# Odd weight units of the later experts issued by ScalarE instead of SP

## The reference

```
def swiglu(h, w1, w3, w2):
    return (jax.nn.silu(h @ w1) * (h @ w3)) @ w2

def moe_swiglu(h, w_router, w1, w3, w2):
    ...
    for e in range(N_EXPERTS):
        y = y + combine[:, e:e + 1] * swiglu(xt, w1[e], w3[e], w2[e]).astype(jnp.float32)
```

## Time and profile before

| | |
|---|---|
| median of 3 runs | 1173.23 us (1171.65 to 1173.63) |
| the profiled execution's own time | 1173.44 us |
| its span, first to last instruction | 1171.5 us |
| PE busy | 1093.9 us (93%) |
| DVE, ACT, POOL busy | 328.6 us, 236.7 us, 39.4 us |
| read from HBM | 414.09 MB |
| issues of expert weights | 195, all by SP |

### The profile page before, as it was taken

The page is one execution under the profiler, slowest core; times in us unless marked ns, Lnnn a source line. Parts: engine busy times, 40 slices in busy tenths (PEclk is TensorE's granted clock), DMA queues, the critical chain, the costliest instruction groups (busy, mean ns, idle before and its releaser), DMA issues.

```text
span 1171.5 us, 25180 instructions
## 1 busy us (share of the span) xinstructions
PE 1093.9 (93%) x11721; PEld 626.0 (53%) x11721; DVE 328.6 (28%) x435; ACT 236.7 (20%) x370; POOL 39.4 (3%) x35
## 2 busy tenths in 40 slices
PE   7999999999999999999989969899997889999776
PEld 6888888889763354354446315344632434364234
DVE  4655555458660030040021004002200310040023
ACT  5676555656620000000000000000000000000002
POOL 3000000011000000000000000000000000000000
PEclk9999999999999999999999999999999899999988
DMA  9985656533379999999999999999999999999994
GB/s 347 387 294 191 203 182 202 191 126 142 134 305 402 422 382 424 428 420 426 424 428 422 426 428 420 427 425 427 421 426 426 424 423 426 427 422 425 426 424 166
DMA packets 58562, 417.88 MB, mean 357 GB/s; under 512 B 5730, under 2 KB 11924, under 8 KB 34004
## 3 DMA queue, kind: packets, MB, share of 16 engines
q1 hardware_dynamic: 56656, 411.21, 86.3%
q0 software_dynamic: 1440, 4.46, 1.0%
q10 hardware_dynamic: 356, 0.54, 0.1%
HBM read 414.09 MB, written 2.10 MB: 355 GB/s over the span
## 4 chain that ended last, share of the span: by engine, by line
PE 70%; DMA 26%; DVE 3%; ACT 1%; SPq 0%; issue 0%; DVEq 0%
PE psum L865 26%; DMA weights<-in_moe_w 26%; PE psum L903 15%; PE psum L771 8%; PE psum L772 8%; PE psum L773 8%; DVE hid_t L1715 1%; DVE sil L1713 1%; PE psum L986 1%; PE psum L844 0%; PE psum L779 0%; DMA x_res<-in_x 0%; PE psum L1107 0%; PE psum L880 0%; PE psum L1084 0%
## 5 line engine op out<-in xcount | busy, mean ns | idle before, releaser
L865 PE MATMUL psum<-weights,xg 128*32 128x512 f32 (+1 forms) x5072 | 494.4, 549 | 47.0 <-DMA weights<-in_moe_w 47.0
L865 PEld LDWEIGHTS psum<-weights,xg 128*32 128x32 f32 x5072 | 181.2, 111 | 357.9 <-issue 321.6
L903 PE MATMUL psum<-weights,hid_t 128*32 128x256 f32 x4480 | 247.1, 380 | 12.4 <-DVE hid_t L1715 8.3
L903 PEld LDWEIGHTS psum<-weights,hid_t 128*32 128x32 f32 x4480 | 151.4, 110 | 104.7 <-issue 13.7
L1713 DVE TENSOR_TENSOR sil<-sil,psum 128x1536 f32<-128x1536 f32 (+3 forms) x16 | 21.1, 1321 | 494.2 <-PE psum L865 493.5
L1567 DVE TENSOR_TENSOR low<-raw,high 128x2048 fp32r<-128x2048 f32 x50 | 114.3, 2286 | 95.5 <-ACT high L1271 95.3
L1271 ACT ACTIVATE high<-raw 128x2048 fp32r<-128x2048 f32 x51 | 97.8, 1917 | 51.8 <-PE psum L773 51.0
L1337 ACT ACTIVATE y_hi<-psum 128x768 fp32r<-128x768 f32 (+1 forms) x7 | 5.0, 719 | 489.4 <-PE psum L903 489.4
L771 PE MATMUL psum<-high,a_hi 128*128 128x512 f32 x224 | 87.2, 389 | 0.9 <-DVE a_lo L1604 0.9
L773 PE MATMUL psum<-low,a_hi 128*128 128x512 f32 x224 | 87.2, 389 | 0.0
L772 PE MATMUL psum<-high,a_lo 128*128 128x512 f32 x224 | 87.1, 389 | 0.0
(11 more groups left out here) (244 smaller groups left out, 662.0 us busy)
## 6 DMA issues: line engine op xcount, KB each, us to landing
weights<-in_moe_w SPq DMA_DIRECT2D x128, 1792.0 KB, 35.1
weights<-in_moe_w SPq DMA_DIRECT2D x47, 2048.0 KB, 37.1
raw<-in_ffn_w SPq DMA_DIRECT2D x42, 1024.0 KB, 7.2
weights<-in_moe_w SPq DMA_DIRECT2D x16, 1024.0 KB, 37.1
raw<-in_w_q SPq DMA_DIRECT2D x4, 1024.0 KB, 5.2
raw<-in_w_o SPq DMA_DIRECT2D x4, 1024.0 KB, 5.0
weights<-in_moe_w SPq DMA_DIRECT2D x4, 512.0 KB, 35.0
x_res<-in_x SPq DMA_DIRECT2D x2, 512.0 KB, 5.3
```

Source lines behind the costliest of these rows:

```text
L865: mm = pe.matmul(UP[c][g * BLK:(g + 1) * BLK, r, :], xg[:, k_, r * BLK:(r + 1) * BLK], w[:, g], start=k_ == 0, stop=k_ == DT - 1)
L903: mm = pe.matmul(Y[g * BLK:(g + 1) * BLK, to, :], hid_t[c][:, r, at_:at_ + BLK], w[:, b, g * GW:(g + 1) * GW], start=i == 0 and b == 0 and ...
```

## The change

From e1 on ScalarE issues the odd units (1, 3, ..., 21), except 21 of e7, on its own queue, and SP skips them. SP keeps e0 whole, the even units, and the last two units of e7. ScalarE issues in two lists for each place e: before the Silu of e those units that become free while TensorE uses the units up to 6 of e, and after the two Silus those that become free by the end of e. Each load waits for the same count of `unit_used` as before, and each list first reads the expert's number from `slot_expert`.

```
+def on_scalar_queue(e, j):
+
+    return e >= 1 and j % 2 == 1 and not (e == E - 1 and j >= MU - 2)
+
+
+def freed_between(first, last):
+
+    return [(n // MU, n % MU) for n in range(E * MU)
+            if on_scalar_queue(n // MU, n % MU) and first < MOE_FREED[n] - U_MOE <= last]
...
                 for j, key in enumerate(MOE_UNITS):
+                    if not ps.block and on_scalar_queue(e, j):
+                        continue
...
+            def load_odd_units(ps, first, last):
+
+                who_of = {}
+                for e, j in freed_between(first, last):
+                    if e not in who_of:
+                        act.wait_ge(slots_known, 1)
+                        who_of[e] = act.value_load(slot_expert[0:1, e:e + 1], min_val=0, max_val=E - 1)
+                    act.wait_ge(unit_used, ps.freed(j, e))
+                    cols = slice(0, moe_size(j))
+                    act.dma_start(expert_tile(ps, j, e, cols),
+                                  expert_source(who_of[e], *MOE_UNITS[j], cols)).then_inc(moe_landed[j], 16)
+
             def expert_feed_forward(ps, e):
                 ps.later(act, e, take_previous)
                 nb = ps.blocks(e)
+                if not ps.block:
+                    load_odd_units(ps, e * MU, e * MU + 7)
                 act.wait_ge(hidden_lo, ps.chunks(0, e))
...
+                if not ps.block:
+                    load_odd_units(ps, e * MU + 7, (e + 1) * MU)
```

## The result

The changed kernel took 1177.26 us in the median of 6 runs (1175.88 to 1177.91), the kernel before 1172.98. The ratio is 1.0042, with a 95% interval of 1.0031 to 1.0052: slower by 4.3 us between these medians, a small change but clear of noise. Forecast was 1179.0 us, that is 5.8 more than before. One of the six runs of before, at 1885.08 us, was disturbed and is left out of the ratio; without it the median of before is 1172.73. The profiled execution took 1177.91 us with a span of 1176.1, 4.6 more than before's.

A forecast was written before the change was run, and what follows sets the result against it. The prediction took the full DMA (share 1.01) to bound the expert part. Issue cost and rate counted nothing; late units added 5.8 us to the profiled 1173.44, giving 1179.2, or 1179.0 us against the median; range 1171.0 to 1187.0 us.

The forecast's parts named there:

- What bounds the kernel: Expert part, 425 to 1125 us: DMA share 1.01, TensorE 57 us to spare; end is landing of units 14, 15 plus 35.8 us.
- ScalarE's work at no cost: ScalarE's queue: 76 issues, 25 us in all over 740 us, and 21 reads of the expert's number, costed at nothing.
- The rate unchanged: Weight loads from 425 to 1125 us: DMA share stays 1.01 and rate 425 GB/s, within some 0.5%; no change in time.
- faster rival: Weight loads: two queues reach 428 GB/s and order holds, 5.1 us less, 1168.1 us; chance of faster 0.14.
- rival three: Weight loads: alternating queues costs what mixing with gathers cost, up to 8.7 us on top of 5.8, up to 1187.7; chance 0.13.
- rival one: Whole kernel: nothing measurable, 1173.2 us within 2.3; needs unit 14 at most 2.3 us late, 16 at most 6.5; chance 0.20.
- Unit 16 late, and so the end: End of the last expert: ScalarE's later units overtake SP's even ones, end 5.8 us later, bounds nothing to 9.8; chance 0.53.
- if both land before 16, it is late by 9.8 us: Last expert's w2: units 17 and 19 land before 16, at 1138.85 instead of 1129.05 us; TensorE ends 5.6 us later.
- unit 14 is overtaken by 17, and by part of 19: End of the last expert's w3: 17 and a quarter of 19 (1.2 us) overtake 14; pair and end 6.1 us later.
- The signs named: Changed profile: SP's units land after 40 us or more, ScalarE's 10 to 25; unit 14 about 1130, last w2 about 1139.
- How the lead arises: Weight queues: SP has 2.1 MB more per place, ScalarE gains one unit, 4.9 us, each; up to 20 us after four places.

The follow-up runs named there:

- e1: Not a run: the second expert place in the kernel, after the one SP keeps whole; the change's ScalarE loads begin here.
- run with 74 loads on ScalarE: The changed kernel with units 17 and 19 of the last expert back on SP's queue; 1171.89 us, ratio to before 0.9998; its rate was 423 GB/s.
- run with e7 alone: Against the kernel before, ScalarE takes the odd units of the last expert only, 10 loads instead of the change's 76; 1179.74 us, ratio 1.0068.
- changed kernel's second profile: The changed kernel run once more, unaltered, beside two others on the same chip; 1176.93 us, ratio to before 1.0034.
- e2: Not a run: the third expert place in the kernel, the one straight after e1; its units 0 and 1 were issued at 500.20 us.
- strict alternation: The changed kernel with odd and even units swapping queues from one expert to the next, so two units in a row are never SP's; 1175.05 us, ratio 1.0027.

## Why the prediction was right, and where it wasn't

**What bounds the kernel** held: DMA share 1.01 after as before, and the end set by what follows the last loads that TensorE must wait for.

**ScalarE's work at no cost** held. Silu waits for TensorE as before, and no wait of TensorE for Silu stands in the changed kernel's profile from 425 us to the end of the experts. The run with 74 loads on ScalarE costs nothing beyond its interval, which shows it. In the run with e7 alone TensorE does wait 0.88 us for a Silu, but that Silu waited for TensorE, not behind a load.

**The rate unchanged** held within its 0.5%: 424 against 425 GB/s, and the run with 423 had before's time. Neither the faster rival nor rival three came true. That spreading doesn't help the rate, as the Trainium skill has it (DMA: Bandwidth & Descriptors, rules for kernel authors), agrees with these rows; that it leaves the time alone, which I made rival one from it, doesn't: the order of landing, with what the clock did behind it, costs 4.3 us.

**Unit 16 late, and so the end** held in direction and place. Three sizes were off.

First, "if both land before 16, it is late by 9.8 us": unit 19 didn't, it landed 3.7 us after 16, so 16 was late by 6.0. Less 4.2 of slack this is a w2 start 1.85 us later, not 5.6. (The prediction also has 19 released after unit 10 is used; it is after unit 9, which ended at 1101.8 us before, just ahead of the issue of 19 at 1101.97.)

Second, "unit 14 is overtaken by 17, and by part of 19": the pair came 1.1 us late, not 6.1, since 17 was only partly there at 1125.3. In both the sum has all of 17 land ahead of 14, as if ScalarE's queue held nothing else by then. Unit 15, on the same queue, landed only at 1119.6, and 17 took 24.7 us from issue to landing.

Third, a term was missing: the wait for 16 was followed by the lower clock, 2.72 us in the profiled execution. The pair, on the other hand, which before ran at the lower clock for part of its 8.08 us, took 6.22 now; that gained nothing, since TensorE had to wait for 16.

So the forecast's size was in part luck. The sum of the profiled parts, 4.57 us, is near the 5.8 because a term too large and a missing one partly cancel. What is more, the prediction's own condition for rival one was met in this execution: unit 14 no more than 2.3 us late (1.1) and 16 no more than 6.5 (6.0). By lateness alone it would have lost 1.85 us, which the prediction counts as nothing measurable. In the changed kernel's second profile the shares are others, 3.10 us of later start and 1.69 of slower matmuls; lateness varies from one execution to the next.

**The signs named** came in part. Unit 14 was the later of the pair, and TensorE waited for each second unit. But SP's units took 30.0 us, not 40 or more, for the prediction didn't reckon with TensorE's later releases; the pair landed at 1125.3 and not near 1130, and w2 started at 1135.12 and not near 1139.

**How the lead arises** was half wrong. "After some four places the odd units are there up to 20 us early" takes the 2.1 MB per place for the source and asks for time. In e1, from 445 to 480 us, the two queues were still level, at 14.0 and 15.5 us. The change has the lead at the second place already: of the two loads issued at 500.20 us, units 0 and 1 of e2, SP's, behind the two halves of unit 22, took 38.5 us and ScalarE's 26.8.

```profile
weights<-in_moe_w SPq DMA_DIRECT2D x4, 1792.0 KB, 14.0
weights<-in_moe_w ACTq DMA_DIRECT2D x4, 1792.0 KB, 15.5
...
weights<-in_moe_w SPq DMA_DIRECT2D x1, 1792.0 KB, 38.5
weights<-in_moe_w ACTq DMA_DIRECT2D x1, 1792.0 KB, 26.8
```

What a queue holds when a load is issued decides, as the run with e7 alone shows. The unequal division is one way to make the queues unequal, and strict alternation ends it (30.2 against 29.6 us).

None of the kernels tried is faster than before beyond the interval.

## What to carry to other kernels

Where one queue already keeps the DMA engines full and a consumer takes the transfers in order, a single queue delivers them in that order; in these runs a second queue brought no more bytes in the same time and moved later units ahead of the one that was waited for. Look at the end of the stream: count which later transfers can overtake the last ones that are followed by compute alone, and compare with the slack of that compute. If two queues are wanted for another reason, let one queue have the end: that alone removed the loss here, while strict alternation took away only part of it (ratio 1.0027 against 1.0042).

## What the runs showed of the hardware that was not expected

GpSimd's gathers took longer beside two busy hardware queues than beside one: over all 17 the median from issue to landing was 7.2 us before and 9.3 in the changed kernel.

```profile
xg_rows<-x_rows,smalls POOLq DMA_INDIRECT x17, 7.2
xg_rows<-x_rows,smalls POOLq DMA_INDIRECT x17, 9.3
```

The other kernels with two queues from e1 on have 9.1 to 10.0 us. The one with e7 alone has 7.3 over all, but 9.2 for its two gathers between 1030 and 1090 us, when ScalarE's queue was at work. TensorE waited for none of them.

Of the clock: after 2.74 us of idling, with the same work before, the 64 matmuls of the pair took the 6.22 us that the 64 before them took (the granted clock in the pair was 1.00), while after 3.59 us the next 128 ran at 0.50 for their first 5.48 us. In the run with unit 19 on SP the 128 matmuls took 8.80 us after idling for only 2.02 us directly before them, so in these rows the length of the last wait alone doesn't decide.

Lastly, hardly any issue blocks now. Before, SP's longest at line 677 was 5.518 us, and at the quarters of unit 22 all four took 3.572 us or more. With half of the units in another queue the longest at the same loop was 0.476 us, ScalarE's longest 0.397, and only one issue of weights, of a quarter of unit 22, was held up (5.808 us).

```profile
L695 SPq DMA_DIRECT2D weights<-in_moe_w x4: 332/333/5808, 1119.7 to 1121.3; - x4
```
